# Linear-attention stage of a decoder step: even and odd heads in turn, sample states loaded into a freed weight slot, softmax sums inverted before they are broadcast

## What is computed

```python
def step(s, inp):                       # GLA, one chunk: 64 tokens of the prompt, 16 meta tokens, or 4 of a sample
    qi, ki, vi, gi = inp
    b = jnp.cumsum(gi, axis=2)
    o_inter = jnp.einsum('bhcd,bhde->bhce', qi * jnp.exp(b), s)
    att = jnp.einsum('bhid,bhjd->bhij', qi * jnp.exp(b - b_mid), ki * jnp.exp(b_mid - b))
    att = jnp.where(causal, att, 0.0)
    o_intra = jnp.einsum('bhij,bhje->bhie', att, vi)
    s_new = s * jnp.exp(b_last)[:, :, 0, :, None] + jnp.einsum('bhcd,bhce->bhde', ki * jnp.exp(b_last - b), vi)
    return s_new, o_inter + o_intra
# mixer_output: og = rms_norm(o_gla) * silu(g);  MLA: p = softmax(scores), o = p @ v
```

## Time and profile before

| | |
|---|---|
| median of 3 executions | 1854.77 us (1854.41 to 1863.11) |
| the profiled execution | 1863.0 us, of which the span of instructions 1861.2 us |
| mean granted TensorE clock | 0.927 of 2.4 GHz |
| TensorE (PE) busy | 1690.0 us, 91% of the span |
| VectorE (DVE), ScalarE (ACT), GpSimd (POOL) busy | 754.4, 584.4, 211.3 us |
| end of the projection, first matmul of tile 0's outputs, last turn of stage C | 265.6, 271.71, 381.11 us |
| attention of the prompt | about 496 to 662 us |

### The profile page before, as it was taken

One profiled execution on the slowest core, in us unless ns is written; L12 is line 12 of the kernel. 1 busy time (PEld: TensorE's weight loads), 2 busy tenths in 40 slices (PEclk: granted clock), 3 DMA queues, 4 the chain that ended last, 5 costly groups with the idle time before them and its releaser, 6 DMA issues.

```text
span 1861.2 us, 26218 instructions
## 1 busy us (share of the span) xinstructions
PE 1690.0 (91%) x10609; PEld 1405.0 (75%) x10609; DVE 754.4 (41%) x1272; ACT 584.4 (31%) x1081; POOL 211.3 (11%) x313
## 2 busy tenths in 40 slices
PE   5999989968999988787997999999999998989994
PEld 4989985535666644444786999999999987868783
DVE  7335014445366633334564222222222223464744
ACT  2245210123355544445111222222222223333331
POOL 2010001110330035521110000000000000010101
PEclk9999995569899988888898999999999998999997
DMA  7201101020100044533222111111111105353430
GB/s 242 103 27 46 46 23 49 1 71 1 38 27 1 1 187 156 196 136 137 91 91 81 46 45 45 45 43 43 42 43 44 45 34 193 126 171 126 165 134 26
DMA packets 90896, 147.20 MB, mean 79 GB/s; under 512 B 6330, under 2 KB 63032, under 8 KB 90776
## 3 DMA queue, kind: packets, MB, share of 16 engines
q1 hardware_dynamic: 74970, 92.31, 15.3%
q0 software_dynamic: 15408, 52.30, 8.0%
q10 hardware_dynamic: 432, 1.37, 0.2%
HBM read 130.24 MB, written 15.72 MB: 78 GB/s over the span
## 4 chain that ended last, share of the span: by engine, by line
PE 65%; DVE 5%; ACT 2%; issue 2%; DMA 1%; POOL 0%; SPq 0%; DVEq 0%; ACTq 0%; POOLq 0%
PE ps L208 15%; PE ps L210 15%; PE ps L209 15%; PE ps L1518 4%; PE ps L1538 4%; PE ps L1207 3%; PE ps L1244 2%; PE ps L1564 2%; ACT pastr L1615 2%; PE ps L1038 1%; PE ps L1221 1%; DVE rs L1354 1%; DVE d_lo L2169 1%; PE ps L1230 1%; DVE y L306 1%
## 5 line engine op out<-in xcount | busy, mean ns | idle before, releaser
L210 PE MATMUL ps<-h1T_hi,f_lo 128*128 128x358 f32 (+1 forms) x1056 | 344.5, 326 | 0.0
L209 PE MATMUL ps<-h1T_lo,f_hi 128*128 128x358 f32 (+1 forms) x1056 | 344.3, 326 | 0.0
L208 PE MATMUL ps<-h1T_hi,f_hi 128*128 128x358 f32 (+1 forms) x1056 | 343.4, 325 | 0.0
L208 PEld LDWEIGHTS ps<-h1T_hi,f_hi 128*128 128x128 f32 x1056 | 199.3, 189 | 0.0
L210 PEld LDWEIGHTS ps<-h1T_hi,f_lo 128*128 128x128 f32 x1056 | 199.3, 189 | 0.0
L209 PEld LDWEIGHTS ps<-h1T_lo,f_hi 128*128 128x128 f32 x1056 | 199.1, 189 | 0.0
L208 PE MATMUL ps<-d_hi,g_hi 128*128 128x512 f32 x396 | 159.2, 402 | 19.0 <-DVE d_lo L2169 16.2
L209 PE MATMUL ps<-d_lo,g_hi 128*128 128x512 f32 x396 | 158.3, 400 | 0.0
L210 PE MATMUL ps<-d_hi,g_lo 128*128 128x512 f32 x396 | 158.0, 399 | 0.0
L208 PE MATMUL ps<-w_hi,hT_hi 128*128 128x256 f32 (+2 forms) x504 | 141.5, 281 | 0.0
L210 PE MATMUL ps<-w_hi,hT_lo 128*128 128x256 f32 (+2 forms) x504 | 140.9, 280 | 0.0
(11 more groups left out here) (294 smaller groups left out, 2848.4 us busy)
## 6 DMA issues: line engine op xcount, KB each, us to landing
d_raw<-in_w_down SPq DMA_DIRECT2D x66, 512.0 KB, 3.5
f_raw<-in_w_ffn_in SPq DMA_DIRECT2D x88, 256.0 KB, 3.1
w_raw<-in_w_in SPq DMA_DIRECT2D x6, 1024.0 KB, 5.2
xs<-in_x_prompt SPq DMA_DIRECT2D x8, 512.0 KB, 3.9
h_res<-xs POOLq DMA_DIRECT2D x8, 512.0 KB, 3.1
wo_raw<-in_w_o SPq DMA_DIRECT2D x2, 2048.0 KB, 9.4
hr<-h_res SPq DMA_DIRECT2D x8, 512.0 KB, 3.6
h_res<-hr POOLq DMA_DIRECT2D x8, 512.0 KB, 3.0
```

The source lines that it names most:

```text
L208: nc.tensor.matmul(out, ah, bh, start=start, stop=False)
L209: nc.tensor.matmul(out, ah, bl, start=False, stop=False)
L210: return nc.tensor.matmul(out, al, bh, start=False, stop=stop)
```

## The change

It does the following.

1. Slabs 3 to 8 swap their two slots, so that slab 7 is in slot 1 and slab 8 in slot 0. `s_in` moves to the high part of slot 1 and its load waits for slab 7 instead of slab 8.
2. In `outputs(i)` the loops over heads become loops over m with the even and the odd head in turn: first the two score matmuls of the pair, then the state matmuls, alternating between partitions 0 to 63 (into bank 4) and 64 to 127 (into bank 5). Tile 0's updates alternate in the same way.
3. Tile 0's second pair of `vz` is made by ScalarE, with its own semaphore, and its updates go to banks 4, 5 and 6 (before 3, 4 and 5).
4. `scores(1)` moves ahead of tile 0's updates; `updates(1)` waits for the first pair's states only.
5. From tile 2 on TensorE does `scores(i)`, `outputs(i-1)`, `updates(i)`, `turn(i-2)`, and VectorE `mask(i)`, `squares(i-1)`, `states(i)`, `scale(i-1)`.
6. The load of `w_uq` waits for the store of the sample states (its place now overlaps `s_in`); the last state store has its own semaphore.
7. `row_sums` inverts 128 x 1 or 128 x 2 sums into `rinv`, waits for that, and then broadcasts them with a copy.

```diff
-        W_SLOT = (0, 1, 2, 0, 1, 0, 1, 0, 1)
+        W_SLOT = (0, 1, 2, 1, 0, 1, 0, 1, 0)
-        s_in = at("s_in", [P, 2, DEC_B, GV], E0 + 47168)
+        s_in = at("s_in", [P, 2, DEC_B, GV], E0 + 93184)
+        U_BANKS = ((2, 3, 7), (4, 5, 6))
...
-            sp.wait_ge(group_done, len(groups))
+            sp.wait_ge(group_done, last_group[7] + 1)
...
-                for h in range(GH):
-                    p, m = GK * (h % 2), h // 2
-                    bank, o = 4 + h % 2, P * (h // 2)
-                    nc.tensor.matmul(ps[0:r, bank, o:o + GV], att[i % 2][:, h % 2, m, 0:r], ...)
+                for m in range(2):
+                    o = P * m
+                    for e in range(2):
+                        nc.tensor.matmul(ps[0:r, 4 + e, o:o + GV], att[i % 2][:, e, m, 0:r], ...)
                     if i == 0:
                         for b in range(DEC_B):
-                            last = nc.tensor.matmul(ps[0:ROWS0, bank, o:o + GV], qbz[p:p + GK, m, b, :], ...)
+                            for e in range(2):
+                                p = GK * e
+                                last = nc.tensor.matmul(ps[0:ROWS0, 4 + e, o:o + GV], qbz[p:p + GK, m, b, :], ...)
                     else:
                         for c in range(2):
                             slot = (2 * (i - 1) + c) % 4
-                            last = nc.tensor.matmul(ps[CH * c:CH * c + CH, bank, o:o + GV], ...)
+                            for e in range(2):
+                                p = GK * e
+                                last = nc.tensor.matmul(ps[CH * c:CH * c + CH, 4 + e, o:o + GV], ...)
...
-            pe.wait_ge(kdt_out, 1)
+            scores(1)
             for m in range(2):
-                pe.wait_ge(vz_ready, m + 1)
-                if m == 1:
+                if m == 0:
+                    pe.wait_ge(vz_ready, 1)
+                else:
+                    pe.wait_ge(vz_act, 1)
                     pe.wait_ge(osb_ready, 2)
-                for hh in range(2):
-                    p = GK * hh
-                    for s0, n in ((0, 4), (4, 4), (8, 1)):
-                        last = nc.tensor.matmul(ps[p:p + GK, 3 * m + s0 // 4, 0:n * GV], ...)
+                    pe.wait_ge(kdt_out, 2)
+                for j, (s0, n) in enumerate(((0, 4), (4, 4), (8, 1))):
+                    for hh in range(2):
+                        p = GK * hh
+                        last = nc.tensor.matmul(ps[p:p + GK, U_BANKS[m][j], 0:n * GV], ...)
                 last.then_inc(u_done, 1)
             for i in range(1, NT + 2):
+                if 2 <= i < NT:
+                    if i == 2:
+                        pe.wait_ge(state_ready, 2)
+                    scores(i)
+                if 1 <= i - 1 < NT:
+                    outputs(i - 1)
                 if i < NT:
                     if i == 1:
-                        pe.wait_ge(state_ready, 2)
-                    scores(i)
+                        pe.wait_ge(state_ready, 1)
                     updates(i)
-                if 1 <= i - 1 < NT:
-                    outputs(i - 1)
...
             kdt_copy(0)
+            for s in range(9):
+                last = nc.scalar.activation(vz[1][:, s, :, :]..., v_t[0:ROWS0, 0, 256:512],
+                                            ACT.Identity, scale=consts[0:ROWS0, C_SEG + s:C_SEG + s + 1])
+            last.then_inc(vz_act, 1)
             o_copy(0)
+            kdt_copy(1)
...
-            for m in range(2):
-                for s in range(9):
-                    last = nc.vector.tensor_scalar(vz[m][:, s, :, :]..., mult)
-                last.then_inc(vz_ready, 1)
+            for s in range(9):
+                last = nc.vector.tensor_scalar(vz[0][:, s, :, :]..., mult)
+            last.then_inc(vz_ready, 1)
+            mask(1)
             squares(0)
...
             scale(0)
-            for i in range(1, NT + 1):
+            states(1)
+            for i in range(2, NT + 1):
                 if i < NT:
                     mask(i)
+                squares(i - 1)
+                if i < NT:
                     states(i)
-                if i >= 2:
-                    squares(i - 1)
-                    scale(i - 1)
+                scale(i - 1)
...
         def sp_d(sp):
-            sp.wait_ge(u_done, 2)
-            sp.wait_ge(state_ready, 2)
+            sp.wait_ge(state_stored, 32)
             sp.dma_start(w_uq[:, :, :, :], ...)
...
-                    last = nc.vector.reciprocal(rs[j % 2][:, :].rearrange("p (e v) -> p e v", e=2),
-                                                rsum[:, a:a + 2, 0:1].broadcast_to((P, 2, VD)))
+                    dve_settle(nc.vector.reciprocal(rinv[:, :], rsum[:, a:a + 2, 0]))
+                    last = nc.vector.tensor_copy(rs[j % 2][:, :].rearrange("p (e v) -> p e v", e=2),
+                                                 rinv[:, :].unsqueeze(2).broadcast_to((P, 2, VD)))
```

More of the change, by code:

```diff
@@ L667, in build @@
         vz_ready = sem("vz_ready")
+        vz_act = sem("vz_act")
         u_done = sem("u_done")
@@ L731, in outputs @@
                     pe.wait_ge(state_ready, 2 + 2 * (i - 1) + 1)
-                for h in range(GH):
-                    p, m = GK * (h % 2), h // 2
-                    bank, o = 4 + h % 2, P * (h // 2)
-                    nc.tensor.matmul(ps[0:r, bank, o:o + GV], att[i % 2][:, h % 2, m, 0:r],
-                                     v_t[:, i, P * h:P * h + P], start=True, stop=False)
+                for m in range(2):
+                    o = P * m
+                    for e in range(2):
+                        nc.tensor.matmul(ps[0:r, 4 + e, o:o + GV], att[i % 2][:, e, m, 0:r],
+                                         v_t[:, i, P * (2 * m + e):P * (2 * m + e) + P], start=True, stop=False)
                     if i == 0:
                         for b in range(DEC_B):
-                            last = nc.tensor.matmul(ps[0:ROWS0, bank, o:o + GV], qbz[p:p + GK, m, b, :],
-                                                    s_in[p:p + GK, m, b, :], start=False, stop=b == DEC_B - 1)
+                            for e in range(2):
+                                p = GK * e
+                                last = nc.tensor.matmul(ps[0:ROWS0, 4 + e, o:o + GV], qbz[p:p + GK, m, b, :],
+                                                        s_in[p:p + GK, m, b, :], start=False, stop=b == DEC_B - 1)
                     else:
@@ L744, in outputs @@
                             slot = (2 * (i - 1) + c) % 4
-                            last = nc.tensor.matmul(ps[CH * c:CH * c + CH, bank, o:o + GV],
-                                                    qb[p:p + GK, m, c0 + CH * c:c0 + CH * c + CH],
-                                                    sst[slot][p:p + GK, m, :], start=False, stop=True)
+                            for e in range(2):
+                                p = GK * e
+                                last = nc.tensor.matmul(ps[CH * c:CH * c + CH, 4 + e, o:o + GV],
+                                                        qb[p:p + GK, m, c0 + CH * c:c0 + CH * c + CH],
+                                                        sst[slot][p:p + GK, m, :], start=False, stop=True)
                 last.then_inc(o_done, 1)
@@ L764, in pe_c @@
             outputs(0)
-            pe.wait_ge(kdt_out, 1)
+            scores(1)
             for m in range(2):
-                pe.wait_ge(vz_ready, m + 1)
-                if m == 1:
+                if m == 0:
+                    pe.wait_ge(vz_ready, 1)
+                else:
+                    pe.wait_ge(vz_act, 1)
                     pe.wait_ge(osb_ready, 2)
-                for hh in range(2):
-                    p = GK * hh
-                    for s0, n in ((0, 4), (4, 4), (8, 1)):
[L773 to L776, removed]
+                    pe.wait_ge(kdt_out, 2)
+                for j, (s0, n) in enumerate(((0, 4), (4, 4), (8, 1))):
+                    for hh in range(2):
+                        p = GK * hh
+                        last = nc.tensor.matmul(ps[p:p + GK, U_BANKS[m][j], 0:n * GV], kdt[0][0:ROWS0, m, p:p + GK],
+                                                vz[m][:, s0:s0 + n, hh, :], start=True, stop=True)
                 last.then_inc(u_done, 1)
             for i in range(1, NT + 2):
+                if 2 <= i < NT:
[4 more added lines that the diff above has]
+                    outputs(i - 1)
                 if i < NT:
                     if i == 1:
-                        pe.wait_ge(state_ready, 2)
-                    scores(i)
+                        pe.wait_ge(state_ready, 1)
                     updates(i)
-                if 1 <= i - 1 < NT:
-                    outputs(i - 1)
                 if i == 1:
@@ L821, in act_c @@
             kdt_copy(0)
+            for s in range(9):
+                last = nc.scalar.activation(vz[1][:, s, :, :].rearrange("p h e -> p (h e)"), v_t[0:ROWS0, 0, 256:512],
```

(6 more changed lines are left out.)

22 lines of the change are left out of this document (12 added, 10 removed).

## The result

| | before | after |
| --- | --- | --- |
| time, median of 4 runs | 1855.9 us | 1801.0 us (1798.7 to 1805.9) |
| ratio | 1 | 0.970, 95% interval 0.967 to 0.973 |
| profiled execution: time, span | 1863.0, 1861.2 us | 1801.2, 1799.4 us |
| mean granted TensorE clock | 0.927 | 0.952 |

The account below looks back on a forecast made before the run. TensorE was taken to bound the kernel nearly everywhere, stage C at 1.2 GHz. Stage C 27.3, clock 4.9 and inversion 8.5 sum to 40.7 us, giving 1814 from the median of 1854.8; range 1801 to 1828, chance 0.8.

Parts of the forecast that it names:

- it stays at 2.4 through the tiles too: Rival: stage C's tiles hold 2.4 GHz, period 5.4 us, 2.1 less on six tiles; 1801 us, chance 0.15.
- the clock's term: Start of stage C: 2.4 GHz back before outputs(0) ends, lost at 285 to 292; 4.9 us more gain.
- State load: Before outputs(0): load comes 9 groups earlier and is hidden; the mask then gates, so outputs(0) starts 2.2 us earlier, at 269.5.
- outputs(0) in pairs: Tile 0 of stage C: the two row halves run side by side, 9.2 us instead of 16.6, 7.4 less.
- The new wait: TensorE ahead of turn(0): idles about 2.3 us at the low clock until scale(0) ends, replacing the old wait.
- The clock at the start: In outputs(0): 2.4 GHz returns before its end, then is lost in waits for VectorE at 285 to 292; 4.9 us.
- The tiles: Stage C's tiles after the start: 7.5 us each instead of 9.83, at 1.2 GHz; gain 14.1 us from scores(3) on.
- The period: Tile period at 2.4 GHz under the high-clock rival: VectorE's 3.5 plus outputs' 1.9 make 5.4 us; chance 0.15.
- The order of the tile: In a tile: outputs cover the key copy, so transposes run straight on, 0.62 us instead of 1.16.
- Narrow inversion: Softmax sums in the prompt's attention: 0.46 us instead of 0.945 each, on 17 to 18 jobs, 8.5 us less.
- The slower rival: Stage D left at the low clock by stage C's earlier end; 60 us of it would give 1874; chance 0.04.

Follow-up runs that it names:

- g3_late_load: Kernel after with the sample state load issued after the last group again; 1907.5 us on a chip where the kernel after took 1903.5.
- f2_tiles_by_head: Kernel after with outputs of tiles 1 to 8 head by head again, outputs(0) still in pairs; 1827.1 us.
- f4_old_order: Kernel after with the old order of a tile from tile 2 on (updates before outputs, states before squares); 1805.0 us.
- g4_after_again: Kernel after, unaltered, run again on another chip; 1903.5 us.
- h1_gate_late: Kernel after with VectorE's gate multiply moved behind the states; 1895.2 us where the unaltered kernel after took 1905.6.
- h2_after_twice: Kernel after, unaltered, run again on a third chip; 1905.6 us, ratio to the kernel before 0.975.
- h3_all_by_head: Kernel after with all outputs by head and tile 0's updates by column half; new order, early load, narrow inversion kept; 1940.8 us.
- g1_before_pairs: Kernel before with outputs of all tiles in pairs and nothing else; 1911.1 us against 1956.9, ratio 0.977.
- f1_wide: Kernel after with the wide inversion of the softmax sums back; 1815.4 us.
- g2_before_narrow: Kernel before with the narrow inversion and nothing else; 1947.9 us, ratio 0.996.
- f3_tile0_by_head: Kernel after with outputs(0) by head and tile 0's updates by column half again, tiles 1 to 8 in pairs; 1815.7 us.

## Why the prediction was wrong, point by point

The time came out at 1801.0, at the lower end of the range and where its own rival "it stays at 2.4 through the tiles too" put it, to which 0.15 was given. The step that failed is the clock's. After outputs(0) the prediction has the clock "lose it again in the waits for VectorE at 285 to 292", and leaves it there: all tiles are summed at 1.2 GHz, with 7.5 us each, and the clock's term is only the 4.9 us of the start. The clock came back in the tiles, at 293.7, and a tile takes 5.64 us. That rival's sum has 53.3 us for stage C and the inversion (40.7 and six times 2.1); measured are 52.6 (2.1, 40.6 and 9.9). So its time was right for its reason, though the last us of the agreement are chance, by the executions' spread (1798.7 to 1805.9).

- *State load.* Right: 2.1 us earlier, for 2.2 forecast, and the mask is what is late next. g3_late_load gives 1.9.
- *outputs(0) in pairs.* Right at either clock. The first pair takes 4.6 us at 1.2 GHz (270.86 to 275.43), as worked out, and the whole 7.5 with the clock's return at 276.6, where 8 to 9 was expected. The two row halves overlap fully. The Trainium skill (TensorE: Matmul & The Clock Gate, Measured speedup vs the span model) gives 3.07 times for four row tiles and nothing for two; as an estimate from that, two would lose something too. With two halves no such loss is in the trace: 32 records in 3.65 us where 16 took 3.65.
- *The new wait.* Right: 1.83 us ahead of turn(0), which starts at 287.34 where 287.5 was forecast. The moment agrees by luck: outputs(0) started 1.4 us later than forecast (270.86 for 269.5), and the stretch from there took 16.5 us for 18.0.
- *The clock at the start.* Back within outputs(0), as forecast. It was lost at 283.4, but not in those waits: PE had been busy without a break since 270.86, the last 4 us in tile 0's updates, and the first wait (0.89) came only then. In f2_tiles_by_head, f4_old_order, g3_late_load, g4_after_again, h1_gate_late and h2_after_twice it fell in the waits, at 281.7 to 287.2. Why it fell earlier in after is open.
- *The tiles.* Wrong. The clock returned at 293.7, after outputs(1) had kept both halves at work at 1.2 GHz, fell at 297.1 after a wait of 1.64 us, and held from 300.5 to 331.2. From turn(0) to the last turn it took 52.3 us (287.34 to 339.67), where 61.5 was forecast (287.5 to 349): these 9.2 us are most of the 10.5 by which the start and the stage gave more (42.7) than the sum had for them (27.3 and 4.9). The argument against it was that "nothing in 109 us of stage C brought it back before". That was true of outputs by head, and the edit replaced just those; the prediction drew that very conclusion for outputs(0) and not for the tiles. f2_tiles_by_head and h3_all_by_head show the low clock with heads, g1_before_pairs the high one with pairs and nothing else.
- *The period.* At 2.4 GHz it is VectorE's chain plus outputs, as the rival said: 3.74 from the end of outputs to the next (310.64 to 314.38) for 3.5, 1.90 for 1.9, 5.64 for 5.4. h1_gate_late confirms that chain.
- *The order of the tile.* The order's cover for the key copy (0.54 us) was counted as a gain. At 2.4 GHz it trades the waits for the key copy and for scale (0.47 and 0.85) for one of 1.46, and gains 0.3 us a tile (5.64 for 5.93 in f4_old_order).
- *Narrow inversion.* Right: 8.5 forecast; 9.9 in the attention of the two profiled executions, 9.2 in f1_wide, 9.0 and 8.6 in g2_before_narrow. PE's idle behind it fell by only 5.3 us (6.8 to 1.5), so the idle alone would have told too little.
- *Not forecast.* The samples' attention is 5.5 us shorter, though nothing in it changed. Its time at 1.2 GHz is 69.0 us before, 55.2 after and in f4_old_order, 65.8 in f1_wide, 59.4 in f2_tiles_by_head. With 221.87 us in both after and f4_old_order, 223.26 in f2_tiles_by_head, 226.79 in f1_wide and 227.36 before, length and low clock go together from kernel to kernel, but no run shows what the clock there hangs on, so how much of it is the change's stays open. It is also why totals here differ by some us more than stage C does.
- *The slower rival.* Its sign, more time at 1.2 GHz between the transposes of w_uk and the first score, did not come: 14.7 us after, 21.2 before.

The Trainium skill (TensorE: Matmul & The Clock Gate, What's actually happening) says that activity releases the clock. These runs agree with it where outputs go in pairs. For outputs by head the busy time of the profile does not tell: 30.00 of 30.00 us counted busy stayed at 1.2 GHz.

## What to carry to other kernels

Where matmuls use 64 of the 128 rows, issue them in pairs on the two halves; look first at the clock's column, since a stage that is busy throughout at 0.50 has as much to gain there as in its overlap. When an argument says "the clock never came back in this stage", ask whether the work that kept it down is the work that the change replaces. And once TensorE runs twice as fast, redo the sum with the other engines' chain: moving one 0.7 us operation out of that chain took 0.73 us off each tile, where the whole reordering took 0.3.

## What the runs showed of the hardware

- TensorE busy without a break does not mean 2.4 GHz: 30.00 of 30.00 us busy in f2_tiles_by_head stayed at 1.2, while 21.45 of 30.70 in the kernel after ran at 2.4.
- Pairs are not at 2.4 GHz from the start either: in f4_old_order PE was busy for 15.05 of 16.00 us in tiles in pairs at 1.2 GHz (284 to 300), and the clock rose only at 309.0.
- What the clock did after an idle differed from trace to trace. Six traces have the tile of the kernel after, with an idle of 1.46 or 1.47 us in each period of 5.64: after kept 2.4 GHz through four of them in a row, g3_late_load and g4_after_again lost it 1.7 us behind the fourth, and f1_wide, f3_tile0_by_head and h2_after_twice once or twice among them. The idle of 1.62 to 1.79 us ahead of outputs(2) was followed by 1.2 GHz in all five traces that have it (after, f1_wide, g3_late_load, g4_after_again, h2_after_twice), and in after the clock was down behind the one of 2.47 (331.29). In h1_gate_late idles of 0.73 to 1.05 us were followed by no fall.
- Two 64-row matmuls on the two halves of the rows cost what one did: 32 records in 3.65 us, where one head's 16 took 3.65, both at 1.2 GHz.
- A reciprocal of 128 x 2 took 157 ns and one of 128 x 128 945; a copy of 128 x 128 took 229.
- Chips differ: the same kernel after took 1801.0, 1903.5 and 1905.6 us on three of them. Stage C was 69.5 to 69.8 on each; the prompt's attention was 162.7, 209.0 and 210.9, the samples' 221.9, 277.0 and 278.2. Part of it is in the traces: in each of the seven of the other two chips TensorE stands still once for 30.6 to 37.3 us in the first jobs of the prompt's attention (33.9 in g4_after_again, ahead of L1234 and put down to ScalarE's copy at L1303), and the samples' attention has 109 to 128 us at 1.2 GHz instead of 55 to 69. No trace of the first chip has that stop. Its cause is open.
